# Feed-forward convolution of a decoder layer: the first tap of three is computed by ScalarE in the next pair's first product, the other two stay on VectorE

## The reference

```python
def conv_ffn(x, buf, w_up, conv_w, w_down):
    u, v = jnp.split(x @ w_up, 2, axis=-1)
    uc, new_buf = causal_dwconv(u, buf, conv_w)      # sum over j of ext[:, j:j+T] * w[j], j = 0, 1, 2
    return (jax.nn.gelu(uc) * v) @ w_down, new_buf
```

## Time and profile before

| | |
|---|---|
| median of 3 runs | 3359.2 us (3358.45 to 3359.69) |
| the profiled execution, its own time | 3366.29 us |
| its span in the trace | 3364.5 us |
| busy PE, DVE, ACT, POOL | 91%, 65%, 35%, 16% of the span |
| mean granted clock of PE | 0.954 of full |
| stretch of the up-projection's pairs in the trace | about 1876 to 2778 us |

### The profile page before, as it was taken

One profiled execution on the slowest core, in us unless ns is written; L12 is line 12 of the kernel. 1 busy time (PEld: TensorE's weight loads), 2 busy tenths in 40 slices (PEclk: granted clock), 3 DMA queues, 4 the chain that ended last, 5 costly groups with the idle time before them and its releaser, 6 DMA issues.

```text
span 3364.5 us, 57012 instructions
## 1 busy us (share of the span) xinstructions
PE 3066.7 (91%) x23903; PEld 2909.8 (86%) x23903; DVE 2190.5 (65%) x3449; ACT 1164.0 (35%) x2020; POOL 521.6 (16%) x294
## 2 busy tenths in 40 slices
PE   7999998988988768998997899999999997898985
PEld 7999988987866547787997899999999997897985
DVE  3111877716655442566558888888888887787877
ACT  2000333105634321343224444444444444344342
POOL 2333333324360110110331000000000000000000
PEclk7999999999999887999998999999999999999998
DMA  6744245419731462123535244444444446434332
GB/s 192 221 131 125 64 130 161 136 50 303 237 138 36 169 249 85 46 87 101 147 89 165 69 124 124 124 124 124 124 121 118 121 124 206 132 127 140 96 109 104
DMA packets 505128, 443.70 MB, mean 132 GB/s; under 512 B 33168, under 2 KB 453936, under 8 KB 497950
## 3 DMA queue, kind: packets, MB, share of 16 engines
q1 hardware_dynamic: 477544, 345.28, 35.4%
q0 software_dynamic: 17488, 75.78, 6.0%
q10 hardware_dynamic: 9840, 19.00, 1.5%
HBM read 377.39 MB, written 70.93 MB: 133 GB/s over the span
## 4 chain that ended last, share of the span: by engine, by line
PE 33%; DVE 11%; DMA 4%; issue 2%; SPq 2%; ACT 1%; DVEq 0%; ACTq 0%
PE i L2542 26%; PE i L129 6%; DVE f_half L2974 3%; DMA s_blk<-x_sums 3%; SPq L2393 1%; DMA x_stage<-s_blk 1%; DVE x_blocks L3012 1%; DVE u_conv L2900 1%; DVE f_sum L2956 1%; ACT f_half L2733 1%; ACT x_blocks L2787 0%; DMA h_rows<-s_h 0%; DVE y_rows L3083 0%; DVE ln_parts L3018 0%; DVE y_rows L3088 0%
## 5 line engine op out<-in xcount | busy, mean ns | idle before, releaser
L2542 PE MATMUL i<-x_blocks,f_half 128*128 128x272 f32 x10752 | 1378.4, 290 | 84.2 <-DVE h_rows L3007 41.8
L2542 PEld LDWEIGHTS i<-x_blocks,f_half 128*128 128x128 f32 x10752 | 1362.1, 190 | 96.8 <-issue 43.5
L2733 ACT CAST f_half<-w_ring 128x1024 fp32r<-128x1024 f32 (+2 forms) x370 | 346.0, 935 | 404.7 <-PE i L2542 348.8
L2974 DVE TENSOR_TENSOR f_half<-w_ring,f_half 128x1024 fp32r<-128x1024 f32 (+2 forms) x362 | 392.8, 1085 | 66.5 <-ACT f_half L2733 63.8
L129 PE MATMUL a<-x_hi,w_hi 128*128 128x272 f32 x1664 | 349.6, 291 | 18.2 <-POOL w_lo L545 18.2
L129 PE MATMUL a<-x_hi,w_lo 128*128 128x272 f32 x1664 | 346.1, 290 | 0.0
L129 PE MATMUL a<-x_lo,w_hi 128*128 128x272 f32 x1664 | 344.8, 289 | 0.0
L545 POOL TENSOR_TENSOR w_lo<-w_ring,w_hi 128x2048 fp32r<-128x2048 f32 x52 | 240.7, 4629 | 455.7 <-DVE w_hi L553 455.7
L129 PEld LDWEIGHTS a<-x_hi,w_hi 128*128 128x128 f32 x1664 | 263.7, 190 | 23.6 <-POOL w_lo L545 22.9
L129 PEld LDWEIGHTS a<-x_lo,w_hi 128*128 128x128 f32 x1664 | 263.3, 190 | 0.0
L553 DVE CAST w_hi<-w_ring 128x2048 fp32r<-128x2048 f32 x52 | 71.4, 1374 | 294.0 <-PE a L129 294.0
(11 more groups left out here) (500 smaller groups left out, 4558.1 us busy)
## 6 DMA issues: line engine op xcount, KB each, us to landing
w_ring<-in_ffn_w_up_dram SPq DMA_DIRECT2D x88, 1024.0 KB, 7.2
w_ring<-in_w_in_dram SPq DMA_DIRECT2D x52, 1024.0 KB, 6.9
w_ring<-in_ffn_w_down_dram SPq DMA_DIRECT2D x24, 1536.0 KB, 7.8
w_ring<-in_w_o_dram SPq DMA_DIRECT2D x16, 1024.0 KB, 6.5
s_blk<-x_sums SPq DMA_DIRECT2D x22, 544.0 KB, 5.9
x_stage<-s_blk SPq DMA_DIRECT2D x14, 816.0 KB, 5.3
s_proj<-x_nat ACTq DMA_DIRECT2D x40, 272.0 KB, 2.7
kv_ring<-in_cmp_w_dram SPq DMA_DIRECT2D x16, 512.0 KB, 8.0
```

Of the source, the lines that this page charges most:

```text
L2542: last = nc.tensor.matmul(ps[bank][:, 0:HT2], half(e, j, wl_)[:, s], XB[:, x0 + s, xl_, BLK_OF[j]], start=start and s == 0 and i == 0, sto ...
L2733: nc.scalar.copy(half(e, j, 0), source(e, j)).then_inc(hq, 1)
L2974: nc.vector.tensor_tensor(half(e, j, 1), source(e, j), half(e, j, 0).bitcast(F32), ALU.subtract).then_inc(lv, 1)
```

## The change

The first of the convolution's three taps, a multiplication by a column of weights, is done by ACT in a new function `first_tap`, as an activation Identity with a scale, once over 512 and once over 32 columns. For tile e + 1 it stands in ACT's order at step (e, 0), behind `high_s`; for tile 0 it stands behind `u_rows(0)`. It takes over the waits of the convolution, the one for `so` among them, and raises `ge`, as the GELU does, so that `ge` counts two for each tile. `conv` on DVE begins with the second tap and waits for `ge` to reach 2i + 1; `gated` waits for 2i + 2.

```diff
--- before.py
+++ after.py
@@ -2716,6 +2716,18 @@
                     nc.scalar.copy(US[:, m, :, 0:2], FB[:, i, 0:SR].rearrange("p (b j) -> p b j", j=2))
                     nc.scalar.copy(US[:, m, :, 2:], ps[4 * i + 1][:, SP2:HT2].rearrange("p (b t) -> p b t", t=T)).then_inc(ue, 1)
 
+                def first_tap(i):
+                    m, w = i % 2, FB[:, i, SR:SR + 1]
+                    if i < NSTD:
+                        act.wait_ge(ue, i + 1)
+                    else:
+                        act.wait_ge(ea, 3 * (i - NSTD) + 3)
+                        act.wait_ge(eb, 3 * (i - NSTD) + 3)
+                    if i >= 2:
+                        act.wait_ge(so, 48 * (i // 2))
+                    nc.scalar.activation(UC[:, m, 0:SEQ], UE[:, m, 0:SEQ], ACT.Identity, scale=w)
+                    nc.scalar.activation(UC[:, m, SEQ:].rearrange("p (b t) -> p b t", t=T), US[:, m, :, 0:T], ACT.Identity, scale=w).then_inc(ge, 1)
+
                 def gelu(i):
                     act.wait_ge(cv, i + 1)
                     nc.scalar.activation(UC[:, i % 2], UC[:, i % 2], ACT.Gelu_apprx_tanh).then_inc(ge, 1)
@@ -2741,6 +2753,7 @@
                 high_half(NO + 3, 0)
                 act.wait_ge(z9, 2)
                 u_rows(0)
+                first_tap(0)
                 high_half(NO + 2, 1)
                 high_half(NO + 3, 1)
                 for s in range(HK):
@@ -2775,6 +2788,8 @@
                         nxt = 7 * e + n + 2
                         if nxt < 7 * NP:
                             high_s(nxt // 7, nxt % 7)
+                        if n == 0 and e <= NU:
+                            first_tap(e + NSTD - 1)
                         if n == 3 and e <= NU:
                             gelu(e + NSTD - 1)
                             if e == NU:
@@ -2882,30 +2897,22 @@
 
                 def conv(i):
                     e, m = i - NSTD, i % 2
-                    if i < NSTD:
-                        dve.wait_ge(ue, i + 1)
-                    else:
-                        dve.wait_ge(ea, 3 * e + 3)
+                    if i >= NSTD:
                         dve.wait_ge(eb, 3 * e + 3)
-                    if i >= 2:
-                        dve.wait_ge(so, 48 * (i // 2))
-                    for j in range(3):
+                    dve.wait_ge(ge, 2 * i + 1)
+                    for j in range(1, 3):
                         w = FB[:, i, SR + j:SR + j + 1]
                         o, x = UC[:, m, 0:SEQ], UE[:, m, j:j + SEQ]
                         os_, xs = UC[:, m, SEQ:].rearrange("p (b t) -> p b t", t=T), US[:, m, :, j:j + T]
-                        if j == 0:
-                            nc.vector.tensor_scalar(o, x, w, None, ALU.mult)
-                            last = nc.vector.tensor_scalar(os_, xs, w, None, ALU.mult)
-                        else:
-                            nc.vector.scalar_tensor_tensor(o, x, w, o, ALU.mult, ALU.add)
-                            last = nc.vector.scalar_tensor_tensor(os_, xs, w, os_, ALU.mult, ALU.add)
+                        nc.vector.scalar_tensor_tensor(o, x, w, o, ALU.mult, ALU.add)
+                        last = nc.vector.scalar_tensor_tensor(os_, xs, w, os_, ALU.mult, ALU.add)
                         link.link(last)
                     nc.vector.tensor_copy(FB[:, i, 0:2], UE[:, m, SEQ:SEQ + 2])
                     nc.vector.tensor_copy(FB[:, i, 2:2 + SR].rearrange("p (b j) -> p b j", j=2), US[:, m, :, T:T + 2]).then_inc(cv, 1)
 
                 def gated(i):
                     e, m = i - NSTD, i % 2
-                    dve.wait_ge(ge, i + 1)
+                    dve.wait_ge(ge, 2 * i + 2)
                     if i < NSTD:
                         dve.wait_ge(mm, NO + 2 + 2 * i)
                         first, second = ps[4 * i + 2][:, 0:HT2], ps[4 * i + 3][:, 0:HT2]
```

## The result

The changed kernel takes 3446.2 us (median of 4 runs, 3439.22 to 3446.49), the kernel before 3359.44 (4 runs, 3358.45 to 3366.49): a ratio of 1.0256, 95% interval 1.0241 to 1.0271, so 81 to 91 us slower. Forecast were 3441 us and a range from 3405 to 3462. The profiled execution took 3446.0 us, its span is 3444.2.

The account below looks back on a forecast made before the run. PE was taken as the bound (busy 435.4 of 440 us). Pauses 70.5 + 0.35, small stops -19.4, clock +32, start -1.0, end -0.7 gave +81.8 us: 3448 against the profiled run, 3441 against the median; range 3405 to 3462.

Parts of the forecast that it names:

- The wait's end, m + 5.32, and the pause: Even tiles: store wait ends 5.32 us after product 0's end (m); PE pauses 3.5 us before product 2, 20 times, 70.5 us.
- The taps, 1.2 us from the wait's end to PE's restart: On ACT behind the store wait: two taps, the copy and PE's start take 1.1 to 1.3 us, taken as 1.2.
- The clock, 32 us: Behind each of 20 PE pauses the clock falls, costing 1.6 us each, 32 us in all (0 to 49).
- (a): Rival: PE pauses the same but returns at full clock, +49.8 us, 3409 us; chance 0.12.
- (b): Rival: two slow clock stretches for each PE pause, 2.44 us instead of 1.6, +98.6 us, 3458 us; chance 0.13.
- The 19.4 us of small stops gone: In the pairs, PE's small stops before product 4 vanish, since DVE's low part of the weights comes in time: -19.4 us.
- rival (c): Rival: the store wait ends early enough to hide in ACT's free time, PE's stops go: -21 us, 3338 us; chance 0.05.
- Start of the stage, 1.0 us: On tile 0, DVE's taps held by POOL's pieces; moving the first tap to ACT saves 1.0 us.
- End of the stage, 0.7 us: In pair 42 the shorter convolution stands ahead of the x_blocks piece PE waits for: 0.67 us saved.
- the store can't come sooner: SP issues the store when the sums over both tiles are done; product 0 of the next pair ends 4.2 us later.

Follow-up runs that it names:

- wait_only: The kernel before, all three taps on DVE, with only ACT's wait for the store added at step (e, 0): 3417.18 us, ratio 1.0176.
- tap_at_step_1: The changed kernel with the first tap and its store wait one step later on ACT, behind the read-out of product 0: 3366.29 us, ratio 1.0021.
- tap_own_buffer: The changed kernel with the first tap written to its own buffer, so ACT waits for no store and DVE does: 3352.34 us, ratio 0.998.
- filled_pause: The changed kernel with six unused float32 matmuls on PE between product 1 and product 2's wait in every odd pair: 3415.03 us, ratio 1.0159.
- store_first: The changed kernel with SP issuing the store of two finished tiles ahead of the same step's 2 MB of weights: 3349.67 us, ratio 0.9976.
- before_conv_step_2: The kernel before with all three taps on DVE one step later, behind the low part of product 4's weights: 3360.28 us, ratio 1.0001.

## Why the prediction was right

It named the place, the chain and the size before the run. That the sum (81.8) came within 2 us of the growth of the profiled run (79.7) is in part luck: pauses and clock were 5.5 us too large, the start and the end of the stage brought 1.3 us less than forecast, 4.6 us had no term, and the profiled run was 2.4 us ahead before the stage for no reason that the change gives. By its own steps:

- **The wait's end, m + 5.32, and the pause.** Forecast 20 pauses of 3.5 us and one of at most 0.7; measured 20 that sum to 67.5 (3.38 each) and one of 0.66. wait_only shows that the wait alone makes pauses of 2.56 us, tap_at_step_1 and tap_own_buffer that it does so by the read-out queued behind it.
- **The taps, 1.2 us from the wait's end to PE's restart.** Measured 1.25. The large tap took 0.72, within 0.62 to 0.79. The Trainium skill (ScalarE: Activation LUTs, "What ACT_TABLE_LOAD costs") gives about 280 ns + 0.833 ns for each column for an activation with one column operand, an estimate of 0.71 and 0.31 us for the two. The trace agrees with 0.72 and 0.30. The small tap is 0.1 us dearer than the copy that I took for its likeness.
- **The clock, 32 us.** Measured 29.2 from the runs of 336, and filled_pause gives 25.6 us back, with 0.9 us of pause left on average (15.8 us in 18). Rivals (a) and (b) are out: of 20 pauses 16 were followed by a fall, which cost about 1.55 us in ten cases and up to 2.8. So the loss was not 1.6 at every pause, but somewhat more at four in five, and that every one of the 20 pauses is dear, as the prediction had it, is not so. It also argued against (a) that the stops of before other than the one of 2.1 us were under 1 us. One of them was 1.53 (at 2165.80), and the clock held behind it (336 matmuls in 42.42).
- **The 19.4 us of small stops gone.** Right in the sum, since in the changed kernel PE's later restart leaves DVE enough time before product 4; the view of before had put all of it on the wait. For its use in rival (c), as what a relief of DVE would win, it was more than twice too large: tap_own_buffer got 8.5.
- **Start of the stage, 1.0 us.** 0.4 in the trace: the third read-out of pair 0 stands 25.6 us behind the last plain matmul's start, 26.0 before. The taps of tile 0 did go by POOL's pieces, as forecast: DVE's second tap, its small one and the third took 1.37, 2.38 and 2.81 us (0.75 us for a large one elsewhere).
- **End of the stage, 0.7 us.** Nothing: from the third read-out of pair 41 to the product with tile 43 (DVE, `gated`) it is 44.6 us in the changed kernel and 44.7 before. The convolution is shorter, but it starts at the landing of h_rows, which came later (DVE idle 10.33 for it, 9.63 before).
- **Rival (c), faster by 21.** It needed stores 3.5 us earlier. store_first brings them about that much earlier, and the changed kernel is then faster than before, by 5 to 11 us. The mechanism was real, its condition was not met, and SP's order was the reason. The prediction wrote that the store can't come sooner. The issue can't, since the sums end just ahead of it, but the landing could: the prediction took it as given and did not ask what lay ahead of it on the queue.

Open are what decides whether the clock falls behind a pause, why before_conv_step_2 takes 2.7 us more behind the stretch, and what the rest of the 4.6 us is.

## What to carry to other kernels

When work moves to an idle engine, its waits move with it, and the engine's idle share says nothing about them: list what is queued behind the new wait up to the next thing that the bound engine needs, and put the wait behind that. Here one step in the order was worth 81 us, and the relief itself about 8. Before a wait for a DMA is moved about, look at what was issued ahead of that DMA: two lines changed places on the queue, and the wait hardly mattered any more.

## What the runs showed of the hardware

- **Short pauses, a slower clock.** Pauses of PE of 2.5 to 4.6 us were followed by a stretch at the lower of the two clock levels in 16 of 20 cases, and length alone did not decide it: behind 3.59 us the clock held (42.16), behind 2.60 and 2.49 it fell (43.71 and 43.72 for 336 matmuls). Length does tell something. In wait_only the clock held behind eleven pauses of 1.58 to 2.68 us and fell behind eight of 2.59 to 3.44, and the kernel before has a fall behind 2.10 (43.72) and none behind 1.53 (42.42).
- **An issue that waits.** The same DMA instruction on SP took 0.34 us with nothing large ahead of it and 2.44 us in the median, up to 4.5, behind two loads of 1 MB. The last DMA of the same store, issued in 0.50 us either way, landed 4.1 us behind its issue in the one case and 5.9 in the other. Why the issue takes longer, no run shows.

The two rows of the kernel before, behind 1.53 and behind 2.10 us:

```profile
2165.80 42.42 PE L2542 MATMUL i<-x_blocks,f_half 128*128 128x272 f32 x336 [1.53 <-DVE f_half L2974]
...
2381.30 43.72 PE L2542 MATMUL i<-x_blocks,f_half 128*128 128x272 f32 x336 [2.10 <-DVE f_half L2974]
```
